# A hybrid decoder layer on one core: FoX's scores and logits two bodies ahead, its maxima taken by the instruction that reads the scores, its causal mask added by GpSimd, and the first products placed among the x transposes

## The reference

```python
h = rms_norm(x, ln_mix[l])
(fq, fk, fv, ff, sz, sxbc, ..., hg) = split_columns(h @ w_in[l], IN_SPLITS)

def forgetting_attention(q, k, v, f_logit, q_norm, k_norm, o_norm):   # 4 heads of 64
    cum_log_f = jnp.cumsum(jax.nn.log_sigmoid(f_logit), axis=1)       # one number per token and head
    for start in range(0, t, FOX_BLOCK):                              # FOX_BLOCK = 128 queries
        end = start + FOX_BLOCK
        logits = jnp.einsum('bqhd,bkhd->bhqk', q[:, start:end], k[:, :end]) * scale
        logits = logits + cum_log_f[:, :, start:end, None] - cum_log_f[:, :, None, :end]
        causal = pos[start:end, None] >= pos[None, :end]
        probs = jax.nn.softmax(jnp.where(causal, logits, MASK_VALUE), axis=-1)
        outs.append(jnp.einsum('bhqk,bkhd->bqhd', probs, v[:, :end]))
    o = rms_norm(jnp.concatenate(outs, axis=1), o_norm)
```

## Time and profile before

| | |
|---|---|
| median of 3 runs | 1726.24 us (1726.07 to 1726.41) |
| the profiled execution, time | 1726.06 us |
| its span | 1724.3 us |
| PE busy | 1650.1 us (96%) |
| DVE busy | 823.3 us (48%) |
| ACT busy | 674.8 us (39%) |
| POOL busy | 56.1 us (3%) |
| mean granted TensorE clock | 0.985 of full speed |
| start of x and first products | 0 to 65 us |
| FoX | 297 to 423 us |
| convolution of SSD after it | 423 to 468 us |

### The profile page before, as it was taken

One profiled execution on the slowest core, in us unless ns is written; L12 is line 12 of the kernel. 1 busy time (PEld: TensorE's weight loads), 2 busy tenths in 40 slices (PEclk: granted clock), 3 DMA queues, 4 the chain that ended last, 5 costly groups with the idle time before them and its releaser, 6 DMA issues.

```text
span 1724.3 us, 20575 instructions
## 1 busy us (share of the span) xinstructions
PE 1650.1 (96%) x8070; PEld 1324.0 (77%) x8070; DVE 823.3 (48%) x1267; ACT 674.8 (39%) x1203; POOL 56.1 (3%) x112
## 2 busy tenths in 40 slices
PE   6999999999897989999999999999999999999997
PEld 5787676676675658788888888888888888888886
DVE  5314633666758455443353245555434455555332
ACT  5214217567433463443333134444423344443221
POOL 2000210000101200000000000000000000000000
PEclk9999899999899999999999999999999999999999
DMA  5122000000201226000021033333222434332222
GB/s 149 49 50 38 16 23 25 13 25 13 73 25 62 86 101 229 0 25 1 10 71 49 19 104 95 95 95 97 70 93 92 123 98 123 98 98 92 98 98 92
DMA packets 166919, 121.29 MB, mean 70 GB/s; under 512 B 23448, under 2 KB 140456, under 8 KB 166824
## 3 DMA queue, kind: packets, MB, share of 16 engines
q1 hardware_dynamic: 165496, 115.53, 21.9%
q10 hardware_dynamic: 1328, 4.46, 0.7%
HBM read 115.77 MB, written 4.19 MB: 70 GB/s over the span
## 4 chain that ended last, share of the span: by engine, by line
PE 61%; DVE 1%; ACT 0%; issue 0%; DVEq 0%; ACTq 0%
PE tail_b L100 19%; PE tail_b L102 19%; PE tail_b L101 19%; PE tail_b L2321 2%; PE tail_b L2296 1%; PE tail_b L2285 0%; PE tail_b L2308 0%; PE tail_b L2232 0%; DVE tail_wl L1996 0%; PE tail_b L2356 0%; PE tail_b L2440 0%; DVE tail_xs L2031 0%; ACT tail_xs L1831 0%; DVE XR L2159 0%; PE tail_b L2369 0%
## 5 line engine op out<-in xcount | busy, mean ns | idle before, releaser
L2152 DVE TENSOR_TENSOR ff_wl<-ff_wr,ff_wh 128x512 fp32r<-128x512 f32 (+1 forms) x176 | 168.5, 959 | 329.8 <-ACT ff_wh L1939 329.8
L1939 ACT ACTIVATE ff_wh<-ff_wr 128x512 fp32r<-128x512 f32 (+1 forms) x176 | 148.7, 846 | 377.9 <-PE tail_b L102 377.9
L100 PE MATMUL tail_b<-HH,ff_wh 128*128 128x512 f32 x704 | 273.9, 389 | 0.0
L101 PE MATMUL tail_b<-HL,ff_wh 128*128 128x512 f32 x704 | 273.9, 389 | 0.0
L102 PE MATMUL tail_b<-HH,ff_wl 128*128 128x512 f32 x704 | 273.9, 389 | 0.0
L100 PE MATMUL mix_gb<-HH,mix_wh 128*128 128x512 f32 x432 | 185.6, 430 | 12.0 <-DVE mix_wl L838 6.6
L101 PE MATMUL mix_gb<-HL,mix_wh 128*128 128x512 f32 x432 | 172.7, 400 | 0.0
L102 PE MATMUL mix_gb<-HH,mix_wl 128*128 128x512 f32 x432 | 172.5, 399 | 0.0
L100 PE MATMUL tail_b<-tail_wh,HH 128*128 128x512 f32 x384 | 153.8, 401 | 6.0 <-DVE tail_wl L1996 4.8
L101 PEld LDWEIGHTS tail_b<-HL,ff_wh 128*128 128x128 f32 x704 | 132.2, 188 | 27.7
L100 PEld LDWEIGHTS tail_b<-HH,ff_wh 128*128 128x128 f32 x704 | 132.2, 188 | 27.4
(11 more groups left out here) (346 smaller groups left out, 2462.8 us busy)
## 6 DMA issues: line engine op xcount, KB each, us to landing
ff_wr<-in_ffn_w_up SPq DMA_DIRECT2D x88, 512.0 KB, 3.6
ff_wr<-in_ffn_w_down SPq DMA_DIRECT2D x88, 256.0 KB, 2.7
mix_wr<-in_w_in SPq DMA_DIRECT2D x26, 512.0 KB, 3.4
mix_wr<-in_xa_wkv SPq DMA_DIRECT2D x16, 512.0 KB, 3.5
XR<-in_x SPq DMA_DIRECT2D x8, 512.0 KB, 6.2
XR<-in_x ACTq DMA_DIRECT2D x1, 4096.0 KB, 18.8
tail_wr<-in_xa_wq SPq DMA_DIRECT2D x16, 256.0 KB, 4.2
tail_wr<-in_xa_wo SPq DMA_DIRECT2D x16, 256.0 KB, 3.4
```

The lines of the kernel that those rows point to most:

```text
L100: pe.matmul(out, hi_w, hi_x, start=first, stop=False)
L101: pe.matmul(out, hi_w, lo_x, start=False, stop=False)
L1939: act.activation(part(FWH[m % FPART], m), part(FWR[m % FRAW], m), ACT.Copy).then_inc(w_hi, 1)
L2152: dve.tensor_tensor(part(FWL[m % FPART], m), part(FWR[m % FRAW], m), part(FWH[m % FPART], m), ALU.subtract)\
```

## The change

It has five parts.

1. TensorE's first four halves of steps are cut in fours: four steps, the transposes of tile 5, four steps, tile 6, four steps, tile 7, four steps. Before, tiles 5 and 6 stood together after half 0 and tile 7 after half 1.
2. In ScalarE's and VectorE's queues `halves(3, 5)` (the copy of half 3, and weight item 3's high and low part) is moved ahead of the wait for the small rows' exponential (`sm_te` on ScalarE, `sm_we` on VectorE).
3. FoX's scores and logits run two bodies ahead instead of one. The scores of body u+2 stand after the transposes of body u.
4. The logits are made, negated, by a `tensor_tensor_reduce` that also takes the row's minimum of what it wrote. The row's own gate term is left out, since it is the same for the whole row and the softmax does not depend on it. The keys' gate rows `CB` are stored negated; for the last 128 keys GpSimd has added the mask to them (`CBM`), so the last piece is cut in a plain and a masked part. A `tensor_reduce` over two or three partial minima of both heads replaces the two masks and the two row maxima. The exponential gets `scale=-1.0`.
5. ScalarE loads the set that has both Ln and Exp by hand ahead of FoX.

```diff
@@ first products and x transposes (TensorE) @@
             pe.wait_ge(E("x_lo"), NT)
-            halves(0, 1)
-            x_transposes(NT // 2 + 1)
-            x_transposes(NT // 2 + 2)
-            halves(1, 2)
-            x_transposes(NT // 2 + 3)
+            for j in range(3):
+                fill(4 * j, 4 * j + 4)
+                x_transposes(NT // 2 + 1 + j)
+            fill(12, 16)
             pe.wait_ge(E("x_lo"), 2 * NT)
@@ small rows (ScalarE; VectorE alike, ahead of sm_we) @@
+            halves(3, 5)
             act.wait_ge(E("sm_te"), 1)
             act.activation(MX[0:64, 4, :], MX[0:64, 4, :], ACT.Exp).then_inc(E("sm_we"), 1)
...
-            halves(3, 2 * F0)
+            halves(5, 2 * F0)
@@ GpSimd @@
+            for u, (hp, i) in enumerate(PAIRS):
+                if i == 0:
+                    pool.wait_ge(E("p_ev"), group_of[CUM(hp)[3]] + 1)
+                if u >= 2:
+                    pool.wait_ge(E("neg_max"), u - 1)
+                for hh in range(2):
+                    pool.tensor_tensor(CBM[2 * (u % 2) + hh], CB[2 * hp + hh][:, i * P:(i + 1) * P], NEGQ[:], ALU.add)\
+                        .then_inc(E("cbm"), 1)
@@ ScalarE @@
-                act.activation(half(CB[h], v), M[3 + m % 2][:], ACT.Copy).then_inc(E("p_ev"), 1)
+                act.activation(half(CB[h], v), M[3 + m % 2][:], ACT.Copy, scale=-1.0).then_inc(E("p_ev"), 1)
...
-                    act.activation(sc, sc, ACT.Exp, bias=NM[:, n:n + 1], accum_out=SUM[:, n:n + 1]).then_inc(E("expd"), 1)
+                    act.activation(sc, sc, ACT.Exp, scale=-1.0, bias=NM[:, n:n + 1], accum_out=SUM[:, n:n + 1]).then_inc(E("expd"), 1)
...
+            act.preload_act_table_set(LN_EXP)
             for entry in CUM(0):
                 extra(entry)
@@ logits and maxima (VectorE) @@
+            n_parts = lambda i: i // 4 + (2 if i % 4 else 1)
...
-                        dve.scalar_tensor_tensor(sc[hh][:, c * NW:c * NW + w], M[m % 3][:, 0:w], ST[:, i, 0, h:h + 1],
-                                                 CB[h][:, c * NW:c * NW + w], ALU.add, ALU.subtract)\
-                           .then_inc(E("sc_read"), 1)
+                        last = c == i // 4
+                        plain_w = w - P if last else w
+                        if plain_w:
+                            at = slice(c * NW, c * NW + plain_w)
+                            one_op = dve.tensor_tensor_reduce(sc[hh][:, at], M[m % 3][:, 0:plain_w], CB[h][:, at], -1.0, -NEG,
+                                                              ALU.add, ALU.min, accum_out=NMX[:, u % 2, hh, c:c + 1])
+                        if last:
+                            if plain_w:
+                                one_op.then_inc(E("nm_part"), 1)
+                            dve.wait_ge(E("cbm"), 2 * u + hh + 1)
+                            one_op = dve.tensor_tensor_reduce(sc[hh][:, keys - P:keys], M[m % 3][:, plain_w:w],
+                                                              CBM[2 * (u % 2) + hh], -1.0, -NEG, ALU.add, ALU.min,
+                                                              accum_out=NMX[:, u % 2, hh, n_parts(i) - 1:n_parts(i)])
+                        one_op.then_inc(E("sc_read"), 1)
...
-                for hh in range(2):
-                    n, sc = 2 * u + hh, SC[2 * (u % 2) + hh]
-                    dve.wait_ge(E("sc_read"), piece_of[(u, i // 4, hh)] + 1)
-                    link(dve.tensor_tensor(sc[:, keys - P:keys], sc[:, keys - P:keys], NEGQ[:], ALU.add))
-                    dve.tensor_reduce(NM[:, n:n + 1], sc[:, 0:keys], AX.X, ALU.max, negate=True).then_inc(E("neg_max"), 1)
+                dve.wait_ge(E("sc_read"), piece_of[(u, i // 4, 1)] + 1)
+                dve.wait_ge(E("nm_part"), 2 * sum(1 for v in range(u + 1) if PAIRS[v][1] % 4))
+                dve.tensor_reduce(NM[:, 2 * u:2 * u + 2], NMX[:, u % 2, :, 0:n_parts(i)], AX.X, ALU.min).then_inc(E("neg_max"), 1)
@@ body loop (VectorE) @@
+                inverse_sums(u)
                 if u:
                     fox_out(u - 1)
-                if u + 1 < len(PAIRS):
-                    logits(u + 1)
-                inverse_sums(u)
-                if u + 1 < len(PAIRS):
-                    maxima(u + 1)
+                if u + 2 < len(PAIRS):
+                    logits(u + 2)
+                    maxima(u + 2)
@@ body loop (TensorE) @@
             scores(0, 0)
+            scores(1, 0)
             for u, (hp, i) in enumerate(PAIRS):
-                new = u + 1 < len(PAIRS)
-                if new:
-                    scores(u + 1, 0)
                 if u == 0:
                     fill(*FOX_A[u])
                 transposes(u, 0)
-                if new and PAIRS[u + 1][1] >= 4:
-                    scores(u + 1, 1)
                 if u:
                     fill(*FOX_A[u])
                 if i >= 4:
                     transposes(u, 1)
+                if u + 2 < len(PAIRS):
+                    scores(u + 2, 0)
                 for entry in FOX_AT(u):
                     extra(entry)
                 fill(*FOX_B[u])
+                if u + 2 < len(PAIRS) and PAIRS[u + 2][1] >= 4:
+                    scores(u + 2, 1)
                 outputs(u)
```

13 lines of the change are left out of this document (8 added, 5 removed).

## The result

The changed kernel took 1710.13 us in the median of four runs (1708.04 to 1711.20) against 1726.33 us before, a ratio of 0.9905 (95% interval 0.9888 to 0.9922). The forecast was 1716.0 with a range from 1712.8: the direction was right, and the gain of 16.2 us was larger than the 10.0 forecast and lies outside the range. Measured again later (e5), the ratio was 0.9911 (0.9892 to 0.9931). Three executions of the study stand in no ratio: one of e15's kernel that ran at a granted clock of 0.65 throughout (2761 us), and two of the kernel before that took 1947 and 2084 us.

A forecast was written before the change was run, and what follows sets the result against it. TensorE was taken as the bound, busy 1650 of 1724 us, so only waits and half-clock time could shrink. From 1726.06 us, −1.5 − 5.5 − 1.0 − 2.0 = −10.0 gave 1716.0, range 1712.8 to 1721.

The forecast's parts named there:

- Terms A and B: At the start: waits for x's last low parts (−1.5 us) and half 3's copy, with slow matmuls behind it (−5.5), go.
- B's clock term: Behind the wait for half 3's copy: 1.7 us lost to slow matmuls at clock 0.54 comes back.
- Term C: In FoX: middle waits fall by 1.9 us, the start costs 0.9 more; −1.0 in all, bounds +1.0 and −2.0.
- The start: Start of FoX: the added table load and GpSimd's mask add delay TensorE by 0.9 us, bounds +0.7 and +1.5.
- rival 1: Start of FoX: two short idles of 1.75 and 0.9 us drop the clock, costing 1.7: 1717.7 us; chance 0.2.
- The middle: Middle of FoX: removed loads and two bodies of slack cut TensorE's waits by 1.9 us, leaving 0.5 at body 14.
- Rival 4: In FoX: slow reading instructions make VectorE the bound, delaying from 1.2 us a piece; 1736 us at 1.5; chance 0.03.
- rival 5: In FoX: GpSimd's 32 mask adds, 18 us, stop VectorE, little reaching TensorE: 1717 us; chance 0.2 shared with two other rivals.
- Term D: Behind FoX: the low part comes 1.28 us sooner and 0.7 of clock returns; −2.0, bounds −1.3 and −3.8.
- Rival 2: Behind FoX: the clock stays full despite 2.7 us of wait, another 1.8 back: 1714.2 us; chance 0.08.
- The sum's base: Whole kernel: the terms were subtracted from one profiled execution of 1726.06 us, close to the median 1726.24.

The follow-up runs named there:

- e5: The changed kernel measured again, unchanged: 1709.29 us, ratio 0.9911 to the kernel before.
- e15: The kernel before with only the copy of half 3 and its weight item moved ahead of the exponential's wait: ratio 0.9974.
- e2: The kernel before with FoX's changes and the hand placed table load, without the reordered transposes and the earlier copy of half 3: ratio 0.9961.
- e3: The kernel before with its first transfer waiting for GpSimd's constants, so work begins about 0.8 us later: ratio 1.0005.
- e14: The kernel before with only TensorE's first products placed among the transposes: ratio 1.0001.
- e10: The kernel before with only the hand placed table load ahead of FoX added: ratio 0.9969.
- e8: The changed kernel with the table load behind the gate rows' four copies and GpSimd's first mask add released by the third copy: ratio 0.9923.

## Why the prediction was too small

*Terms A and B* (−1.5, −5.5): the two waits went as worked out, the window from 40 to 62 us shows TensorE without a gap, and the copy of half 4 did not become late. B's clock term was right for the profile that it was read from. Of the five profiles with the wait of 3.79, three lost 1.6 to 1.7 behind it (before, e2, e3) and two 2.7 and 2.9 (e14, e10), mean 2.1. The times give 7.1 for both (4.1 to 9.8).

*Term C* (−1.0): the FoX stage went from 123.9 to 122.1, −1.8. The start was right, +0.95 for +0.9, and so was rival 1's answer: the clock stayed at 1.00 there. The middle was mis-sized and for a partly wrong reason: nothing remained in body 14 (0.5 was left for it), because the gates' Ln had been one of the loads, and the slack of two bodies was given a share that it does not have. By e10 the load does all of it, 2.6 of stage: 1.5 in the listed waits and 1.2 in TensorE's busy time, which term C put at nothing. Parts 3 and 4 give 0.9 of that back.

*Rival 4 and rival 5* did not come: the reading operation took 0.29 to 0.69 us a piece, and VectorE's share fell to 54, below the forecast's 62. (By the forecast's own terms, with the reads at 0, that bound should have been 57.) While GpSimd made its first eight adds (292.92 to 296.40) VectorE's 128-column pieces kept their 0.29 us, and the adds their 0.46. The reading operation has one input in PSUM; the two engines held each other up only where VectorE had both in SBUF, at four of the changed kernel's adds and at the first ones of e8. Rival 5 had its mechanism right, but none of it reached TensorE.

*Term D* (−2.0) was mis-sized: 1.28 of idle as forecast, and between the two first profiles 0.9 of clock, but "I take back 0.7" for the clock should have been 1.9 as a mean over profiles, since the shorter wait most often is followed by no slow matmul at all. Rival 2 (chance 0.08) is what happened in seven of eleven profiles. The one earlier wait of 2.8 followed by slow matmuls, which spoke against it, was one draw: in others the same wait was followed by none.

*The sum's base* is the step that failed. The terms were set against one profile's slow stretches as if those at places that the change does not touch would stay, so their part was put at nothing, and three runs within 0.4 us were taken as the kernel's spread. Of the 18.0 us between the two first profiles 9.2 are idle: 8.2 by the terms' waits, 0.9 behind the last matmul. 7.3 are lost clock (21.1 to 13.8); 2.6 of that was at the places that the change touches (1.7 behind half 3, 0.9 behind FoX), the other 4.7 at untouched ones. Of the 1.5 left, 1.0 is the slow matmuls at the very start, which ended at 25.6 us in place of 27.6 by the starts of the first products, and 0.3 is busy time in FoX. So 4.7 of the 8.0 us by which these two profiles differ more than forecast, and 1.0 at the start, are draws of the clock; that the first comparison lies outside the range is in part luck. With means in place of draws the forecast would be 8.2 idle + 2.1 + 1.9 = 12.2, and 0.3 of busy time in FoX: −12.5, 1713.6. With the 0.9 behind the last matmul it would be −13.4, 1712.7. Measured were −14.5 to −16.4 with 3 us either way. The 1 to 3 us between are not explained by a row, and may be sampling. The range's low end was also short by its own rule: terms C and D at their bounds give 1713.2, where it says 1712.8.

## What to carry to other kernels

Where a wait of TensorE is followed by slow matmuls in one profile, take another execution before pricing it: the price of a wait is its idle plus a chance of half clock. At the place behind FoX that was 0.6 us for 2.68 of idle and 2.5 for 3.96, so shortening the long wait there was worth more than its length. Length alone does not decide: a later wait of 3.4 to 3.8 us for a half's copy (3.43 at 559 us in the kernel before) was followed by no slow matmul in five of nineteen profiles. Before restructuring a pipeline to hide ScalarE's lateness, look for the table loads in its queue; one load placed by hand took away eight in FoX, and with them the waits in its middle that two bodies of look-ahead and a shorter VectorE chain were there for. A clean stage (clock 1.00 in every profile) is the measure for edits of a microsecond: its length repeated within 0.1 us where whole runs of one kernel were up to 10 us apart.
